# Seven weight units of the first attention as three float32r passes, and the modulation products moved from that attention to the recurrent output product and the first feed-forward

## The reference, cut to what matters

```python
h = x
h = h + rg_lru_block(rms_norm(h), ...)              # layer 0: recurrence, 2 x 1024 wide in, 1024 out
h = h + swiglu_ffn(rms_norm(h), ...)                # 1024 -> 2 x 2816 -> 1024
h = h + stick_breaking_attention(rms_norm(h), w_qkv, w_o)   # layer 1: 16 heads of 64
h = h + swiglu_ffn(rms_norm(h), ...)
x = rms_norm(h)
mod = silu(c) @ w_ada + b_ada                       # modulation: 6 x 1024 values from a [1, 1024] row
h = rmsnorm(x) * (1 + sc1) + sh1
...                                                 # two attentions, a gated merge, 32 experts, top-2
```

## Time and profile before

| | |
|---|---|
| median of 3 runs | 1366.44 us (1366.33 to 1366.56) |
| the profiled execution | 1365.0 us, span 1363.2 us |
| PE busy | 1278.1 us, 94% of the span |
| DVE busy | 574.2 us, 42% |
| ACT busy | 370.2 us, 27% |
| DMA, mean | 266 GB/s over the span |
| q, k, v products | from 317.50 to 400.5 us |
| attention loop | from 401.7 to 435.6 us |
| output product | from 435.61 to 463.5 us |

### The profile page before, as it was taken

The page is one execution under the profiler, slowest core; times in us unless marked ns, Lnnn a source line. Parts: engine busy times, 40 slices in busy tenths (PEclk is TensorE's granted clock), DMA queues, the critical chain, the costliest instruction groups (busy, mean ns, idle before and its releaser), DMA issues.

```text
span 1363.2 us, 19682 instructions
## 1 busy us (share of the span) xinstructions
PE 1278.1 (94%) x7758; PEld 943.6 (69%) x7759; DVE 574.2 (42%) x934; ACT 370.2 (27%) x489; POOL 30.9 (2%) x55
## 2 busy tenths in 40 slices
PE   8998999999999899999899999979999999889887
PEld 6887999998847799999799888843333333333332
DVE  3544544445564254555634787461212121211213
ACT  2524333322136143333624565240000000000001
POOL 0000000000000000000000000000000000000000
PEclk9999999999999999999999999979999999999999
DMA  9754555537993535553644433589999999999995
GB/s 349 255 179 139 186 185 185 185 124 294 413 384 126 187 117 180 179 179 117 110 146 166 144 124 132 197 337 392 430 428 428 427 429 427 429 429 428 428 425 215
DMA packets 97730, 362.38 MB, mean 266 GB/s; under 512 B 3968, under 2 KB 51472, under 8 KB 83984
## 3 DMA queue, kind: packets, MB, share of 16 engines
q1 hardware_dynamic: 95376, 335.32, 64.6%
q0 software_dynamic: 2160, 26.24, 4.7%
q10 hardware_dynamic: 144, 0.10, 0.0%
HBM read 360.58 MB, written 1.06 MB: 265 GB/s over the span
## 4 chain that ended last, share of the span: by engine, by line
PE 82%; DMA 11%; DVE 3%; ACT 2%; issue 1%; SPq 0%; DVEq 0%; ACTq 0%
PE ps L1643 19%; PE ps L1591 15%; PE ps L1937 12%; DMA wbuf<-in_w_up 11%; PE ps L1557 9%; PE ps L1987 5%; PE ps L1815 4%; PE ps L1566 4%; PE ps L1957 3%; PE ps L1582 2%; PE ps L1536 2%; PE ps L1575 1%; PE ps L1610 1%; PE ps L1709 1%; DVE big L1471 1%
## 5 line engine op out<-in xcount | busy, mean ns | idle before, releaser
L1643 PE MATMUL ps<-big_parts,parts 128*128 128x256 f32 x2112 | 261.7, 285 | 5.4 <-DVE big_parts L1011 5.1
L1643 PEld LDWEIGHTS ps<-big_parts,parts 128*128 128x128 f32 x2112 | 258.3, 194 | 7.6 <-issue 5.8
L1937 PE MATMUL ps<-wbuf,big 128*64 128x512 f32 x1024 | 226.3, 593 | 11.7 <-DMA wbuf<-in_w_up 11.7
L1011 DVE TENSOR_TENSOR parts<-wbuf,parts 128x2048 fp32r<-128x2048 f32 x66 | 150.9, 2292 | 135.7 <-ACT parts L653 75.1
L1937 PEld LDWEIGHTS ps<-wbuf,big 128*64 128x64 f32 x1024 | 83.0, 137 | 150.7 <-issue 135.7
L1987 PE MATMUL ps<-wbuf,big 128*64 128x512 f32 x512 | 118.6, 604 | 19.7 <-DVE big L1471 19.7
L1557 PE MATMUL ps<-big,wbuf 128*128 128x256 f32 x576 | 127.0, 383 | 3.8 <-ACT big L633 2.2
L1591 PE MATMUL ps<-big_parts,parts 128*128 128x256 f32 x1056 | 130.0, 283 | 0.0
L1591 PEld LDWEIGHTS ps<-big_parts,parts 128*128 128x128 f32 x1056 | 128.2, 192 | 0.0
L935 ACT ACTIVATE big<-ps 128x256 f32<-128x256 f32 x31 | 11.9, 384 | 418.9 <-PE ps L1937 418.9
L1557 PEld LDWEIGHTS ps<-big,wbuf 128*128 128x128 f32 x576 | 110.5, 192 | 19.8 <-issue 4.5
(11 more groups left out here) (306 smaller groups left out, 1346.8 us busy)
## 6 DMA issues: line engine op xcount, KB each, us to landing
wbuf<-in_w_down SPq DMA_DIRECT2D x32, 2048.0 KB, 26.1
wbuf<-in_w_gate SPq DMA_DIRECT2D x31, 2048.0 KB, 23.3
wbuf<-in_w_up SPq DMA_DIRECT2D x31, 2048.0 KB, 27.8
wbuf<-in_ffn_w_in SPq DMA_DIRECT2D x44, 1024.0 KB, 9.2
wbuf<-in_w_ada POOLq DMA_DIRECT2D x12, 2048.0 KB, 10.5
wbuf<-in_ffn_w_out SPq DMA_DIRECT2D x22, 1024.0 KB, 5.0
wbuf<-in_w_in SPq DMA_DIRECT2D x10, 2048.0 KB, 8.2
wbuf<-in_attn_w_qkv SPq DMA_DIRECT2D x6, 2048.0 KB, 14.1
```

What stands on the lines that cost most here:

```text
L1011: nc.vector.tensor_tensor(lo, whole, hi.bitcast(F32), ALU.subtract).then_inc(done, 1)
L1643: ins = mm(ps[:, b, d * 256:(d + 1) * 256], w[pw][:, k, d * P:(d + 1) * P], h_part_of[px][:, k], start=(k == 0 and i == 0), stop=(k == KC ...
L1937: ins = mm(at, rows, gu_place[s][:, :, k, h * 256:(h + 1) * 256], start=(k == 0), stop=(k == KC - 1))
```

## The change

1. The units `q1 k0 k1 v0 v1 wo0 wo1` join `SPLIT` (as `SPLIT_1`): ACT writes their high parts, DVE their low parts, and PE multiplies in three float32r passes. The normed rows get parts too (`xq_part`), and so does the attention's output (`o_part`: a copy and a subtraction for each pair of heads in place of one copy). `q0` stays plain.
2. The high parts of these units lie where the feed-forward's split weights lie (`wo1`: in the feed-forward's second slot). So the first split of the second feed-forward comes in two pieces, gate after `v0` has been multiplied and up after the high part of `wo1`, and SP loads the second slot only after the product of `wo1`.
3. The modulation comes in 24 loads of 1 MB and groups of 2 rows, into one reserved place ("ada") in the unit ring. POOL begins when `gb1` has been multiplied. DVE multiplies 4 groups before it waits for the recurrent output product, then 2 groups in each feed-forward step (`ADA_FROM`), which is written out as 11 steps and not as a loop. The silu(c) row lies elsewhere and ACT makes it before the first feed-forward.
4. The reserved place shifts all later units by one place. `k0` is loaded after the first feed-forward's loads. Before the experts SP loads the gate of expert 2 first and its down weights last, where it had loaded the down weights first.

```diff
+RING.insert(RING.index("lo1") + 1, "ada")
+SPLIT_AFTER = {"q1": f"ffn0_{FFN_STEPS - 1}", "k0": f"ffn0_{FFN_STEPS - 1}", "k1": f"ffn0_{FFN_STEPS - 1}",
+               "v0": "q1", "v1": "k0", "wo0": "k1", "wo1": "v1"}
+SPLIT_1 = ["q1", "k0", "k1", "v0", "v1", "wo0", "wo1"]
-ADA_UNITS = 12
-ADA_GROUP = 4
-ADA_EARLY = 10
+ADA_UNITS = 24
+ADA_GROUP = 2
+ADA_EARLY = 4
+ADA_FROM = (4, 6, 8, 10, 12, 14, 16, 18, 20, 22, 23)
...
-            for name in ("gb1", "lo0", "lo1", "q0", "q1", "k0"):
+            for name in ("gb1", "lo0", "lo1", "q0", "q1"):
                 load_unit(name)
             load_ffn_rest(0)
             load_ffn_first(1, 0)
-            for name in ("k1", "v0", "v1", "wo0", "wo1", "qm"):
+            for name in ("k0", "k1", "v0", "v1", "wo0", "wo1", "qm"):
                 load_unit(name)
-            sp.wait_ge(ada_used, ADA_UNITS)
+            wait_used(sp, "wo1")
             load_ffn_first(1, 1)
...
             load_down(sp, 0, 0)
-            load_down(sp, 2, 2)
+            load_gate_up(sp, 2, 2, (0,))
             wait_used(sp, "out1")
             load_gate_up(sp, 1, 1)
             load_down(sp, 1, 1)
-            load_gate_up(sp, 2, 2)
+            load_gate_up(sp, 2, 2, (1,))
+            load_down(sp, 2, 2)
...
-            wait_used(pool, f"ffn0_{FFN_STEPS - 1}")
+            wait_used(pool, "rec0")
             pool.dma_start(c_row, a["c_2"].to_broadcast([P, D])).then_inc(c_in, 16)
+            wait_used(pool, "gb1")
...
+            for b in range(4):
+                act.wait_ge(h_ready, 2 * KC + 2 * b + 2)
+                nc.scalar.activation(xq_part[0][:, 2 * b:2 * b + 2], hT[:, 2 * b:2 * b + 2], ACT.Copy).then_inc(fh_hi, 1)
+            for i, name in enumerate(("q1", "k0", "k1", "v0", "v1", "wo0")):
+                hi_unit(name)
+                if name == "wo0":
+                    wait_used(act, "v0")
+                    split_g(0, ffn_loads(1, 0))
+                for t in range(2 * i, 2 * i + 2):
+                    if i < 2:
+                        copy_pair(f"q{t}", qT[:, 2 * t:2 * t + 2], scale=SCALE)
+                    elif i < 4:
+                        copy_pair(f"k{t - 4}", kT[:, 2 * t - 8:2 * t - 6])
+                    else:
+                        copy_pair(f"v{t - 8}", vtok[:, t % 2, (i - 4) * 512:(i - 3) * 512])
...
+            hi_unit("wo1")
+            split_u(0)
             ffn_norm(3, 1)
...
+            dve.wait_ge(silu_c, 1)
+            for u in range(ADA_EARLY):
+                ada_unit(u)
             wait_used(dve, "lo1")
...
+                    if layer == 0:
+                        for u in range(ADA_FROM[n], ADA_FROM[n + 1] if following else ADA_UNITS - 1):
+                            ada_unit(u)
...
+            for b in range(4):
+                subtract(xq_part[1][:, 2 * b:2 * b + 2], hT[:, 2 * b:2 * b + 2], xq_part[0][:, 2 * b:2 * b + 2], fh_hi, KC + b + 1, fh_lo)
+            for name in ("q1", "k0", "k1", "v0", "v1", "wo0"):
+                lo_unit(name)
+            split_g(0, FFN_STEPS)
...
             def o_copy(c):
                 dve.wait_ge(o_done, c + 1)
-                nc.vector.tensor_copy(hT[:, c], ps[:, 4 + c % 2, 0:256]).then_inc(o_evac, 1)
+                link(nc.vector.tensor_copy(o_part[0][:, c], ps[:, 4 + c % 2, 0:256]))
+                nc.vector.tensor_tensor(o_part[1][:, c], ps[:, 4 + c % 2, 0:256], o_part[0][:, c].bitcast(F32), ALU.subtract).then_inc(o_evac, 1)
 
             for c in range(KC):
                 soft_plus(c)
                 if c >= 2:
                     o_copy(c - 2)
-                ada_product(ADA_EARLY + c // ADA_GROUP, c % ADA_GROUP)
             o_copy(KC - 2)
             o_copy(KC - 1)
+            lo_unit("wo1")
+            split_u(0, FFN_STEPS)
...
+            wait_unit(pe, "q0")
+            for h in range(2):
+                product_pair(f"q{h}", unit_view("q0"), 2 * h, KC, hT, 2 if h == 0 else None)
+            pe.wait_ge(fh_lo, KC + 4)
+            for nm, u in (("q", 1), ("k", 0), ("k", 1)):
+                wait_parts(f"{nm}{u}")
+                for h in range(2):
+                    product_pair_parts(f"{nm}{2 * u + h}", unit_parts(f"{nm}{u}"), 2 * h, KC, xq_part)
             for u in range(2):
-                wait_unit(pe, f"v{u}")
+                wait_parts(f"v{u}")
                 for c in range(TC):
-                    token_major(f"v{2 * u + c}", unit_view(f"v{u}"), hT, c)
+                    token_major_parts(f"v{2 * u + c}", unit_parts(f"v{u}"), xq_part, c)
```

More of the change, by code:

```diff
@@ L184, in program @@
         sk = [flat(WORK + 6144 + 768 * i, 768).rearrange("p (h n) -> p h n", h=2) for i in range(4)]
[L185 removed]
+        ident_half, hidden_half = (big_half[:, 2 * 11648 + P * i:2 * 11648 + P * (i + 1)] for i in range(2))
         def z_banks(c):
@@ L333, in unit_parts @@
         def unit_parts(name):
-            k = 4 if name[0] in "po" else KC
-            hi, lo = HI_AT[SPLIT.index(name) % 2], (parts_0, parts_1, parts_2)[RING.index(name) % PLACES]
-            return [region.rearrange("p (k f) -> p k f", k=k) for region in (parts_f[:, hi:hi + UNIT], lo)]
+            k, lo = 4 if name[0] in "pow" else KC, (parts_0, parts_1, parts_2)[RING.index(name) % PLACES]
+            if name in SPLIT_2:
+                at = HI_AT[SPLIT_2.index(name) % 2]
+                hi = parts_f[:, at:at + UNIT]
+            elif name == "wo1":
+                hi = parts_f[:, EXPERT - UNIT:EXPERT]
+            else:
+                at = SPLIT_1.index(name) % 3 * UNIT
+                hi = parts[:, at:at + UNIT]
+            return [region.rearrange("p (k f) -> p k f", k=k) for region in (hi, lo)]
         def halves(v):
@@ L388, in program @@
             s = i % PLACES
-            load_count[name] = (s, 1 + sum(1 for m in load_count if load_count[m][0] == s and m != "gates"))
+            load_count[name] = (s, 1 + sum(1 for m in load_count if load_count[m][0] == s and m not in ("gates", "ada")))
         def wait_unit(eng, name):
@@ L699, in _, with hi_half, hi_unit @@
                 nc.scalar.activation(half, half, ACT.Sqrt).then_inc(mult_done, 1)
+            def hi_half(name, i):
+                n = SPLIT.index(name)
+                if i == 0:
+                    wait_unit(act, name)
+                    if name in SPLIT_1:
+                        wait_used(act, SPLIT_AFTER[name])
+                    elif SPLIT_2.index(name) < 2:
+                        act.wait_ge(fu_lo, 2 * FFN_STEPS - 1 + SPLIT_2.index(name))
+                    else:
+                        wait_used(act, SPLIT[n - 2])
+                nc.scalar.activation(halves(unit_parts(name)[0])[i], halves(unit_view(name))[i], ACT.Copy).then_inc(w_hi, 1)
+            def hi_unit(name):
+                hi_half(name, 0)
+                hi_half(name, 1)
             def ffn_norm(n, layer):
@@ L706, in ffn_norm @@
                     nc.scalar.activation(h_part_of[0][:, k], hT[:, k], ACT.Copy).then_inc(fh_hi, 1)
[L708 to L714, removed]
-                    else:
-                        wait_used(act, SPLIT[n - 2])
-                nc.scalar.activation(halves(unit_parts(name)[0])[i], halves(unit_view(name))[i], ACT.Copy).then_inc(w_hi, 1)
-            def hi_unit(name):
-                hi_half(name, 0)
-                hi_half(name, 1)
             def ffn(layer):
@@ L1069, in lru_gate, with ada_product, ada_unit @@
                 nc.vector.tensor_tensor(gl[:, m], gl[:, m], cv[:, m], ALU.mult).then_inc(y_done, 1)
+            def ada_product(u, j):
+                w, at = ada_place[u % 2][:, j], ADA_GROUP * u + j
+                if j == 0:
+                    dve.wait_ge(ada_loaded[u % 2], 16 * (u // 2 + 1))
+                ins = nc.vector.scalar_tensor_tensor(out=w, in0=w, scalar=1.0, in1=c_row, op0=ALU.mult, op1=ALU.mult, accum_out=ada[:, at:at + 1])
+                if j == ADA_GROUP - 1:
+                    ins.then_inc(ada_used, 1)
+            def ada_unit(u):
+                for j in range(ADA_GROUP):
+                    ada_product(u, j)
             rec_normed(0)
@@ L1133, in step @@
                             lo_unit("km")
+                        else:
+                            ada_unit(ADA_UNITS - 1)
                     dve.wait_ge(ffn_silu, n + 1)
@@ L1143, in step @@
                         lo_unit("vm")
+                    if layer == 0:
+                        for u in range(ADA_FROM[n], ADA_FROM[n + 1] if following else ADA_UNITS - 1):
+                            ada_unit(u)
+                if layer == 0:
+                    for n in range(FFN_STEPS):
+                        step(n % 2, n, following=n + 1 < FFN_STEPS)
+                    return
                 step(0, base)
```

69 lines of the change are left out of this document (26 added, 43 removed).

## The result

The changed kernel took 1351.23 us (median of 4 runs, 1344.97 to 1352.61), the kernel before 1366.38 us beside it (4 runs, 1364.98 to 1366.56). The ratio is 0.9882, with an interval of 0.9851 to 0.9914. Run once more in a later experiment, the same code took 1349.61 us (4 runs, 1345.61 to 1350.78), with a ratio of 0.9891 (0.9874 to 0.9908). The forecast was 1349.4: the first figure is 1.8 us above it, the second 0.2 us. The first lies 0.2 us above the forecast's own range (1348.3 to 1351) and inside the wider one (1346.0 to 1354.5). That the second comes so near is luck: the kernel before took 1364.46 us beside it, not 1366.4, so the gain there is 14.9 us, where 17.0 was forecast. The profiled execution took 1352.61 us, with a span of 1350.8.

A forecast was written before the change was run, and what follows sets the result against it. PE was taken as the bound, holding 82% of the chain (DMA 11%). 17.5 us saved less 0.5 lost gave 1366.44 - 17.0 = 1349.4 us, own range 1348.3 to 1351, wider range 1346.0 to 1354.5.

The forecast's parts named there:

- Three passes: First attention's q1, k0, k1, v0, v1 and output product in three float32r passes: 17.5 us off PE's chain.
- Rival 4: Three passes take three quarters of a plain tile's time in q, k, v and output product: 1342.6 us; chance 0.02.
- Parts ready: First attention: ACT and DVE finish each unit's parts before PE asks, 3.8 us to spare at q1; cost nothing.
- Rival 1: The first attention's weight loads land late, 21.8 us at worst, and PE waits: 1355 us; chance 0.05.
- The last pair of `o_copy`: End of the attention loop: PE waits for the last pair's copy and dependent subtraction; cost 0.46 us, bounds 0.3 and 0.9.
- Modulation: Early groups beside the recurrent output product end at 100 or 108.4, two more hide in each feed-forward step; cost nothing.
- Rival 2: Early modulation outlasts the recurrent output product, DVE ending 9.2 us after PE: up to 1358.6 us; chance 0.06.
- Rival 3: POOL's loads late in first feed-forward steps; PE stalls from a 21 us landing, 1379 us at 24; chance 0.05.
- The experts' start: Last stage, waiting for weights, with expert 2's loads reordered: expected to stay at 484 us.
- Rival 5: Reordered expert loads gain or lose one 2 MB load, 5.2 us, in the last stage: 1344.2 or 1354.6; chance 0.04.
- The sum: Whole kernel: 17.5 us gained less 0.5 lost gives 17.0 us off the run's time, 1349.4 us.

The follow-up runs named there:

- e8: Changed kernel plus 73 constant 128-column PE products in short idle times (norms 1 to 5, attention loop), results unchanged; 1344.77 us, ratio 0.9857.
- e9: Kernel before the change plus the same constant products at the same places (norms 1 to 5, attention loop); 1359.78 us, ratio 0.9971.
- e10: Changed kernel plus constant products in the attention loop alone; 1348.61 us, ratio 0.9880.
- e3: Changed kernel with only v0 and v1 back in plain float32; 1353.32 us, ratio 0.9917.
- e2: Changed kernel with all seven units back in plain float32, modulation left where the change puts it; 1365.12 us, ratio 0.9999.
- e5: Changed kernel with 22 of 24 modulation groups left out, loads and products, the vector set to a constant; 1350.63 us, ratio 0.9901.
- e6: Changed kernel with eight modulation groups instead of four beside the recurrent output product; 1365.68 us, ratio 1.0008.
- e7: Changed kernel with four modulation groups a feed-forward step instead of two; 1384.31 us, ratio 1.0147.
- e1: Changed kernel run once more with no edit; 1349.61 us, ratio 0.9891.

## Why the prediction was right, and what was off

**Three passes.** The six tiles of q1, k0, k1 took 34.54 us against 34.5 forecast, the values 21.80 against 21.9, the output product 23.27 against 23.0. With q0's 14.05 the stage gives 12.6 us, and the output product 4.6, 17.2 together against 17.5. The missing 0.3 is 0.1 in q, k and v and the 0.2 by which this output product is longer than the one of the second attention. Rival 4 falls: a tile of q or k in passes costs 34.54 / 6 = 5.76, 0.83 of a plain one, and the values 21.80 / 27.48 = 0.79. The Trainium skill, page "FP8 and Floating Point Precision", section "TensorE Precision Notes", gives true FP32 four passes. By that count alone three would take 0.75; the trace doesn't agree.

What lies between can be worked out from the same pieces, as an estimate. A tile of q or k is 16 products of 256 columns: a quarter of a plain one is 6.94 / 64 = 0.108 us, a float32r pass 5.76 / 48 = 0.120. The values' products have 512 columns: 27.48 / 128 = 0.215 and 21.80 / 96 = 0.227. In both shapes a pass takes some 12 ns more than a quarter of a plain product, so the wider product comes nearer to 0.75. Why these 12 ns are there, no run shows.

**Parts ready.** PE never waits between 317.27 and 387.6. Rival 1 falls with its cause: the loads landed in 8.5 us in the middle, 12.1 at worst, where 21.8 was the worst beside the modulation. The forecast's 8 was the best of them (8.0), and near enough.

**The last pair of `o_copy`.** 0.46 us was forecast, and 0.46 is what e8 against e9 gives. In the loop as a whole the first profile showed 2.08; the other 1.6 is the low clock after the wait for the first soft plus. e8 and e10 remove it with idle-time products alone, and e3 didn't have it at all.

**Modulation.** The early groups end at 100.7, at the forecast's better bound (100), 9.2 us before the add; the steps stay at 17.28 us and the first feed-forward at 200.38. e2 and e5 say that the move costs nothing. Rival 2 is a real mechanism that doesn't bind here: e6 shows it, and the gain is lost. Rival 3's own condition, a landing of 21 us or more, was far away: 10.4 at worst. e7 shows the wait that it described, DVE late with PE's gate weights, but from another cause: a load inside the step, with no landing over 9.6 us. It costs 20 us more than the kernel before.

The rule of the Trainium skill, page "SBUF — State Buffer", section "SBUF: two separate sides", doesn't show in these rows. In e6, three of POOL's loads (issued at 92.07, 100.02 and 111.06) landed in 5.25, 8.34 and 8.28 us, and each had the same 2.4 us of DVE's products beside it. In the changed kernel, where DVE is busy beside most of them, the median is 8.3. So there is no sign that these products hold POOL's loads up; whether they are the kind of operation that the page means, no run here decides.

**The experts' start.** Rival 5 falls too. In the first profile the stage was 1.73 us longer, in e1 with the same code 0.09 us shorter. The grouped rows of the changed kernel and of e1 show where (idle time before the group at the end):

```profile
L1989 PE MATMUL ps<-wbuf,big 128*64 128x512 f32 x1024 | 226.4, 593 | 13.5 <-DMA wbuf<-in_w_up 13.5
```

```profile
L1989 PE MATMUL ps<-wbuf,big 128*64 128x512 f32 x1024 | 226.4, 593 | 11.8 <-DMA wbuf<-in_w_up 11.8
```

The same work waits 1.7 us more or less for its weights from one execution to the next.

**The sum.** The step that was off is the last one: 17.0 us of PE's chain were taken one for one off the run's time. On the chain the change is worth 16.7 to 16.8 us (e8 against e9), as forecast. The medians moved by 15.15 us, and by 14.9 when e1 is set beside its own runs of before. What lies between is in size like one of the low-clock stretches, which the sum didn't have: the one in the loop cost 1.6 us. The kernel before had none at the start of its loop in its profile (35.14 us), and the changed one had it in both profiles (37.22 and 37.26).

That this stretch is the missing 1.8 us is not shown. For it speaks that of the eight profiles of the changed kernel and its variants without idle-time products, seven have it and only e3 has not. Against it, of the kernel before there is only one such profile, and one can't say how often the stretch comes there. Also the medians of e8 and e9 are still only 15.0 us apart, though neither profile has the stretch. What stays open, then, is where the medians lose 1.7 us against the chain, and whether the loop's start is more prone to the low clock than before: PE waits there for the same ACT and DVE work, and plain products don't prevent it (e2). The mean granted clock of the changed kernel's first four runs, 0.983 to 0.989, is like that of before, 0.984 to 0.989 in the later runs.

## What to carry to other kernels

Where PE's chain is unbroken, price a change of precision by a tile of the same shape in the same trace, not by the count of passes; it held here to 0.3 us in 17.5. Work that is moved under cover (here loads and products of the modulation) costs nothing as long as its whole round of load, wait and use fits, and when it doesn't, PE pays the wait, and a slow stretch behind it where PE's own work is next in the chain (e6, not e7). Before a difference of 1 or 2 us between two profiles is put down to a change, profile one of them twice: here the same code gave 1345.6 and 1352.6.

## What the runs showed of the hardware

The granted clock falls to its lower level for some 3.4 us at a time after idle time of PE, and with the same program it does so at some of the candidate places in one execution and not in the next. At the experts' start it stays there longer (a mean of 0.57 from 862 to 878 us in e8). A stretch in which PE's chain is unbroken costs about 1.5 us (1.6 in the loop, 4.35 for three in the second attention). One in which PE waits for DVE between its products costs nothing (the one at 455.8, 6.3 us behind the norm's start). The one of the kernel before falls 2.4 us later behind its norm, when PE's products run on, and there the second feed-forward takes 200.93 us instead of the 200.38 of e9.

Idle-time products keep the clock up: with 73 of them the mean granted clock went from 0.983 to 0.989 in the changed kernel's runs to 0.991 to 0.993, and the time down by about 5 us, in the kernel before by 4.4 (1364.14 to 1359.78). At 225 ns each they must be fewer than the wait they stand in.

After an idle time of 14.25 us PE's next 16 products took 5.31 us instead of 3.73, and norm and feed-forward 2.0 us more in all (e6). So an idle time in PE's own chain costs that much more than its length. Where another engine's chain sets the pace it does not: in e7, 96 products took 14.07 us instead of 11.68 behind a wait, and no step was longer for it.
